# Modulation slots 8 and up moved from the token projection to the mixers' front, and the two widest masked copies made by ScalarE

## The reference, cut to what matters

```
mod = silu(c) @ w_mod + b_mod            # one row per group: shift, scale, gate (twice), 6 x 1024
h   = rmsnorm(x) * (1 + sc1) + sh1
z   = h @ w_in                            # 2352 columns: latents of the attention, q, k, v, gates of the recurrences
o   = [attention(z), hgrn2(z), gla(z)]    # the three mixers
x   = x + g1 * (o @ w_o)
h2  = rmsnorm(x) * (1 + sc2) + sh2
x   = x + g2 * ((silu(a) * u) @ w_ffn_out),   a, u = h2 @ w_ffn_in
```

## Time and profile before

| | |
|---|---|
| median of 3 runs | 3438.68 us (3432.39 to 3442.31) |
| profiled execution, its own time | 3439.55 us |
| its span, first to last instruction | 3437.7 us |
| PE busy | 3216.9 us, 94% of the span |
| mean granted TensorE clock | 0.975 of full speed |
| token projection of layer 0, of layer 1 | 140.4 to 340.1 us, 1831.4 to 2018.4 us |
| mixers' front of layer 0, of layer 1 | 340 to 444 us, 2018 to 2122 us |

### The profile page before, as it was taken

The page is one execution under the profiler, slowest core; times in us unless marked ns, Lnnn a source line. Parts: engine busy times, 40 slices in busy tenths (PEclk is TensorE's granted clock), DMA queues, the critical chain, the costliest instruction groups (busy, mean ns, idle before and its releaser), DMA issues. The chain is left out here.

```text
span 3437.7 us, 50868 instructions
## 1 busy us (share of the span) xinstructions
PE 3216.9 (94%) x19854; PEld 2901.5 (84%) x19854; DVE 1488.5 (43%) x2525; ACT 983.0 (29%) x2015; POOL 762.6 (22%) x1091
## 2 busy tenths in 40 slices
PE   6999788889999999999989987888899999999999
PEld 5988556666999999999988975666589999999998
DVE  5411446655353334433372124566555334333443
ACT  4212334444331111111152123444434121211211
POOL 4101757631210000000051155665213000000000
PEclk7999999999999999999999999999999999999999
DMA  6565111103111111111125431110221111111111
GB/s 210 183 194 172 55 45 58 39 15 105 62 38 49 37 37 49 50 48 37 37 87 172 148 89 52 46 53 21 61 93 37 37 37 61 49 37 37 37 37 52
DMA packets 191693, 237.04 MB, mean 69 GB/s; under 512 B 18058, under 2 KB 165855, under 8 KB 191551
## 3 DMA queue, kind: packets, MB, share of 16 engines
q1 hardware_dynamic: 176764, 198.29, 17.9%
q0 software_dynamic: 10560, 31.44, 2.7%
q10 hardware_dynamic: 4226, 5.40, 0.6%
HBM read 195.53 MB, written 39.56 MB: 68 GB/s over the span
## 5 line engine op out<-in xcount | busy, mean ns | idle before, releaser
L1560 PE MATMUL banks<-act_split,w_split 128*128 128x384 f32 (+1 forms) x8352 | 1403.6, 329 | 10.6 <-DVE act_split L2293 7.4
L1560 PEld LDWEIGHTS banks<-act_split,w_split 128*128 128x128 f32 x8352 | 1387.0, 189 | 23.2 <-DVE act_split L2293 12.3
L1560 PE MATMUL banks<-hidden_split,w_split 128*128 128x384 f32 (+1 forms) x3168 | 525.0, 326 | 0.0
L1560 PEld LDWEIGHTS banks<-hidden_split,w_split 128*128 128x128 f32 x3168 | 522.3, 188 | 0.0
L2330 DVE SCALAR_TENSOR_TENSOR x<-banks,mod,x 128x384 f32<-128x384 f32 (+2 forms) x768 | 353.4, 497 | 185.6 <-PE banks L1560 183.2
L2768 DVE TENSOR_TENSOR hidden_f<-banks,silu_a 128x384 f32<-128x384 f32 x132 | 70.7, 536 | 736.5 <-PE banks L1560 736.5
L1560 PE MATMUL banks<-w_split_tm,act_split 128*128 128x396 f32 (+1 forms) x1728 | 323.9, 345 | 0.0
L1560 PEld LDWEIGHTS banks<-w_split_tm,act_split 128*128 128x128 f32 (+1 forms) x1728 | 299.2, 182 | 25.6 <-issue 14.0
L1521 ACT ACTIVATE w_split<-w_raw 128x2048 fp32r<-128x2048 f32 x60 | 112.4, 1906 | 381.3 <-PE banks L1560 381.3
L1515 ACT ACTIVATE hidden_split<-hidden_f 128x384 fp32r<-128x384 f32 x132 | 67.1, 508 | 519.6 <-DVE hidden_f L2768 519.6
L621 POOL TENSOR_TENSOR norm_sum_n<-norm_sum_n,norm_sq 128x384 f32<-128x384 f32 (+1 forms) x42 | 43.9, 1048 | 771.8 <-ACT norm_sq L972 766.6
(11 more groups left out here) (233 smaller groups left out, 3424.2 us busy)
## 6 DMA issues: line engine op xcount, KB each, us to landing
w_raw<-in_w_ffn_in SPq DMA_DIRECT2D x44, 1024.0 KB, 5.1
w_mod_raw<-in_w_mod SPq DMA_DIRECT2D x41, 1024.0 KB, 5.4
w_raw<-in_w_ffn_out SPq DMA_DIRECT2D x22, 1024.0 KB, 4.9
z_token_major<-z_stage POOLq DMA_DIRECT2D x64, 198.0 KB, 2.4
r_qkg<-z_feature_major SPq DMA_DIRECT2D x16, 576.0 KB, 4.2
r_v<-z_token_major SPq DMA_DIRECT2D x16, 512.0 KB, 3.6
w_raw<-in_w_o SPq DMA_DIRECT2D x8, 1024.0 KB, 7.1
w_mod_first<-in_w_mod SPq DMA_DIRECT2D x7, 1024.0 KB, 12.4
```

The costliest lines, as they stand in the source:

```text
L1560: return T.matmul(out, lhsT, rhs, start=start, stop=stop, skip_group_check=True)
```

## The change

1. Slots 0 to 7 of layer 0 stay where they are. All others leave the token projection, on PE, DVE and SP. In the front, step i carries slot 8 + i: PE runs `mod_turns(i)` between its piece and `r_slot(i)`, or before the piece in steps 6, 7, 11, 15, 19 and 23. DVE runs the copy and the keeping at the end of its step i. PSUM banks 2 and 3 take the place of 6 and 7 there.
2. The weights of a slot come in two DMAs of 512 KB, into two buffers of their own (`w_mod_front`). Slot 8 is loaded by SP early in the token projection; all others are issued by ACT: slot 9 as the front begins, slot 10 + i at the end of ACT's step i, once PE has made the rows of slot 8 + i.
3. Levels 5 and 6 (b = 32, 64) of all 9 tiles are copied from PSUM to r_p by ACT, in two plain copies of 32 partitions x 256 elements and one of 64 x 512, in place of DVE's two masked copies of 128 x 512 (`wide_level`, in ACT's steps h = 6 and 7). PE's `outputs` and the next users of their banks wait for ACT accordingly.
4. PE waits at the end of the front for the last slot to be kept, and ACT's first softmax exponential for the last rows. SP, POOL and DVE no longer wait for the slots before the front.

```
+WIDE_LV = 5
...
+    def load_mod(eng, l, n):
+        s = 8 + n
+        src = w_mod_v[l + s // NMOD][:, :, 256 * (s % NMOD):256 * (s % NMOD) + 256]
+        for u in range(2):
+            eng.dma_start(MF[n % 2][u].rearrange("p (k c) -> p k c", k=4), src[:, 4 * u:4 * u + 4]).then_inc(mod_ld[n % 2], 16)
...
-                order = [("t", 0), ("t", 1)] + mods[:2] + [("t", 2)] + mods[2:4] + [("t", 3)] + mods[4:11]
-                order += [("w", 9), ("w", 10)] + mods[11:17] + [("w", 11)] + mods[17:]
+                order = [("t", 0), ("t", 1), ("m", 0), ("t", 2), ("t", 3), ("w", 9), ("w", 10), ("w", 11)]
...
+                def wide_level(g, lv):
+                    b = LEVELS[lv]
+                    src = ps[R_BANK[f"s{lv}"]].rearrange("p (h n c) -> p h n c", h=8, c=b)
+                    wait(act, "r_pe", l, f"s{g}_{lv}")
+                    wait(act, "r_dve", l, f"m{g}_{WIDE_LV - 1}")
+                    for n in range(64 // b):
+                        t0 = 2 * b * n
+                        ins = S.activation(rP[t0:t0 + b, :, t0 + b:t0 + 2 * b], src[t0:t0 + b, :, n], ACT.Copy)
...
                     if i:
                         r_slot(i)
+                    if i + 2 < NMOD_L[l]:
+                        act.wait_ge(mod_pe, l * NMOD + 8 + i + 1)
+                        load_mod(S, l, i + 2)
...
-                        pos = 9 * j + p
-                        if pos < 33 and pos % 4 < 3:
-                            mod_turns(pos - pos // 4)
...
                 for i in range(24):
+                    ahead = i == 6 or i % 4 == 3 and i > 3
+                    if ahead:
+                        mod_turns(i)
...
+                    if not ahead:
+                        mod_turns(i)
                     if i:
                         r_slot(i)
+                mod_turns(24)
+                pe.wait_ge(mod_dve, MOD_ALL[l])
...
-                    if g < NTILE and h:
+                    if g < NTILE and 0 < h <= WIDE_LV:
                         masked(g, h - 1)
...
                         k_sum(f"p{(i - 9) // 4}", P)
+                    mod_parts(i)
+                mod_parts(24)
```

More of the change, by code:

```diff
@@ L196, in program @@
     at = [h_at, h_end]
-    MR = place("w_mod_raw", [P, 2, 2048], F32, at)
-    MS = place("mod_rows", [P, 256], F32, at)
+    MR = place("w_mod_raw", [P, 2048], F32, at)
+    MS = place("mod_rows", [P, 256], F32, [h_at + 16384, h_end])
     CST = place("cst", [P, CST_W], F32)
@@ L262, in program @@
     rQB = place("r_qb", [P, 2, 8, 64], F32, a)
+    MSF = place("mod_rows_front", [P, 256], F32, a)
     a = [wr_at + 6144, wr_at + SLOT * 4]
@@ L285, in program @@
     PT = place("probs_t", [P, 2, 4, P], F32, a)
+    MF = [[place(f"w_mod_front{i}{u}", [P, 1024], F32, [o, o + 4096])
+           for u, o in enumerate((h_at, h_at + 4096) if i == 0 else (h_at + 8192, a_at + 43008))] for i in range(2)]
     CT = place("c_t", [P, 4, P], F32, a)
@@ L455, in _ @@
                     load_raw(l, n, wl[:, :, FM_COLS[n]:FM_COLS[n] + 256], 8)
-                mods = [("m", n) for n in range(8, 8 + NMOD_L[l])]
-                order = [("t", 0), ("t", 1)] + mods[:2] + [("t", 2)] + mods[2:4] + [("t", 3)] + mods[4:11]
-                order += [("w", 9), ("w", 10)] + mods[11:17] + [("w", 11)] + mods[17:]
+                order = [("t", 0), ("t", 1), ("m", 0), ("t", 2), ("t", 3), ("w", 9), ("w", 10), ("w", 11)]
                 for kind, n in order:
                     if kind == "m":
[L462 to L466, removed]
+                        wait(sp, "n1_dve", l, "lo27")
+                        load_mod(sp, l, n)
                     elif kind == "t":
@@ L1096, in r_slot @@
                     if g < NTILE:
+                        if h > WIDE_LV:
+                            wide_level(g, h - 1)
                         if h == 0:
@@ L1208, in probs @@
                     wait(act, "a_dve", l, f"mx{t}_{h}")
+                    if q == 0 and h == 0:
+                        act.wait_ge(mod_pe, MOD_ALL[l])
                     if h >= 2:
@@ L1283, in _ @@
                 t8, n8 = ORDER[0], DEC_SEQ
+                load_mod(S, l, 1)
                 decay(0, 0, 0)
@@ L1581, in mod_rows @@
                 def mod_rows(q):
[L1583 to L1586, removed]
-                    else:
[L1588 to L1591, removed]
+                    first = l == 0 and q < 8
+                    if first:
+                        pe.wait_ge(mod_la[q] if q < NMOD_A else mod_l7, 16)
+                        w = [(MA[:, q] if q < NMOD_A else MR)[:, 1024 * u:1024 * u + 1024] for u in range(2)]
+                        bank = ps[3 if q % 2 else 6]
+                    else:
+                        pe.wait_ge(mod_ld[q % 2], mod_ready(l, q - 8))
+                        w, bank = MF[q % 2], ps[2]
                     if q > first:
@@ L1595, in mod_rows @@
                         g = 32 * (k % 4)
-                        ins = mm(ps[3 if first and q % 2 else 6][g:g + 32, 0:256], SCV[:, k, :], w[:, k, :], k < 4, k >= 4)
+                        ins = mm(bank[g:g + 32, 0:256], SCV[:, k, :], w[k // 4].rearrange("p (k c) -> p k c", k=4)[:, k % 4],
+                                 k < 4, k >= 4)
                     ins.then_inc(mod_pe, 1)
@@ L1603, in mod_turn @@
                         pe.wait_ge(mod_dve, l * NMOD + q)
+                    first = l == 0 and q < 8
                     for ct in range(2):
-                        ins = mm(ps[7][:, 2 * ct:2 * ct + 2], MS[:, P * ct:P * ct + P], CST[:, O_SEL:O_SEL + 2],
-                                 True, True)
+                        ins = mm(ps[7 if first else 3][:, 2 * ct:2 * ct + 2], (MS if first else MSF)[:, P * ct:P * ct + P],
+                                 CST[:, O_SEL:O_SEL + 2], True, True)
                     ins.then_inc(mod_sum, 1)
@@ L1785, in outputs @@
                     b = R_BANK["o"]
-                    wait(pe, "r_dve", l, f"m{g}_{NLEV - 1}")
+                    wait(pe, "r_dve", l, f"m{g}_{WIDE_LV - 1}")
+                    wait(pe, "r_act", l, f"m{g}_{NLEV - 1}")
                     pe.wait_ge(rv_ld, (l * NTILE + g + 1) * 16)
@@ L2367, in mod_copy @@
                         dve.wait_ge(mod_sum, l * NMOD + q)
-                    V.tensor_copy(MS[:], ps[3 if l == 0 and q < 8 and q % 2 else 6][:, 0:256]).then_inc(mod_ev, 1)
+                    if l == 0 and q < 8:
+                        V.tensor_copy(MS[:], ps[3 if q % 2 else 6][:, 0:256]).then_inc(mod_ev, 1)
+                    else:
+                        V.tensor_copy(MSF[:], ps[2][:, 0:256]).then_inc(mod_ev, 1)
                 def mod_keep(q):
                     dve.wait_ge(mod_sum, l * NMOD + q + 1)
+                    src = ps[7 if l == 0 and q < 8 else 3][:, 0:4].rearrange("p (k a) -> p k a", k=2)
                     if q >= NMOD:
-                        V.tensor_copy(MODN[:, 2 * (q - NMOD):2 * (q - NMOD) + 2, :],
-                                      ps[7][:, 0:4].rearrange("p (k a) -> p k a", k=2)).then_inc(mod_dve, 1)
+                        V.tensor_copy(MODN[:, 2 * (q - NMOD):2 * (q - NMOD) + 2, :], src).then_inc(mod_dve, 1)
                         return
-                    V.tensor_tensor(MOD[:, 2 * q:2 * q + 2, :], ps[7][:, 0:4].rearrange("p (k a) -> p k a", k=2),
+                    V.tensor_tensor(MOD[:, 2 * q:2 * q + 2, :], src,
                                     PRM[:, 2 * q:2 * q + 2].unsqueeze(2).broadcast_to([P, 2, 2]), ALU.add).then_inc(mod_dve, 1)
@@ L2424, in gate, with mod_parts @@
                     s.done(V.tensor_scalar(ZT3[:, 0:n], ZT3[:, 0:n], 1.0 / TAU, None, ALU.mult), f"g{c}")
-                for p in range(25):
+                def mod_parts(p):
                     if 1 <= p <= NMOD_L[l]:
@@ L2430, in _ @@
                         mod_copy(8 + p)
[L2431 to L2434, removed]
+                split_lo(l, 5, None)
+                split_lo(l, 6, None)
+                for c in range(3):
+                    gate(c)
                 rs = st("r_dve")
                 s = st("a_dve")
-                dve.wait_ge(mod_dve, MOD_ALL[l])
                 def rstep(ins, name, now=False):
```

17 lines of the change are left out of this document (7 added, 10 removed).

## The result

| | before | changed |
|---|---|---|
| median | 3438.68 us | 3459.49 us (3456.76 to 3461.1) |
| profiled execution, its span | 3437.7 us | 3459.3 us |
| mean granted clock | 0.975 | 0.971 |

The ratio is 1.006, with a 95% interval of 1.0045 to 1.0074: the changed kernel is slower by 20.8 us. Forecast were 3436 us with a range up to 3456, so the forecast was wrong.

What follows compares the result with a forecast made beforehand. PE was taken to bound the kernel, busy 3216.9 of 3437.7 us. From 3439.55 us, 58.4 removed and 55.9 taken back by the fronts gave 3437.0, by the median 3436 us, with a range from 3410 to 3456.

Steps and rivals of the forecast that it cites:

- What is removed: Token projections: 24 slots leave layer 0 and 16 leave layer 1, 35.0 + 23.4 = 58.4 us, all on the path.
- The walk of the tile: Front, steps 8 to 15: eight slots worth 11.7 us cost 12.8 us, as a longer PE-DVE-PE loop leaves gaps unfilled.
- a slot is 1.46 us on PE: Front: each slot's turn and rows priced at a mean of 1.46 us on PE.
- The rest of step 15 runs at half clock before and warm behind shorter gaps: 1 us back: Front, end of the tile: late by 13.8 us at k_turn, 1 us won back, so step 16 starts 12.8 us late.
- rival 2: Fronts: slots shorten long waits, so up to half of 38 us at half rate is won, 9 us: 3427 us; chance 0.09.
- The sum: Whole kernel: 3439.55 - 58.4 removed + 55.9 taken back by the fronts = 3437.0, so 3436 us by the median.
- the first tile of layer 1: Front of layer 1, first tile: slots add 8 us, the figure walked for the first tile of layer 0.
- a front over 145 us: Sign of being wrong: fronts exceeding 145 us, and then, by PE's wait on w_mod_front, Rival 3 holds.
- The masked copies: Attention: 36 copies leaving DVE, partly for ACT, costed at nothing; bounds 18 us gained to 14 us lost.
- Rival 1: Fronts grow only by what exceeds the gaps, 7.6 us and nothing: 3388 us, halfway 3412; chance 0.20.
- Rival 3: `mod_rows` in the front: loads landing in 7.4 us instead of 5.4 add 20 us, 3456 us; chance 0.28.

Runs made afterwards that it cites:

- changed_again: The changed kernel itself run once more, unaltered, beside the other runs: 3456.5 us, 1.0054 times the kernel before.
- filled: The changed kernel with 2 to 7 useless matmuls of 256 columns put into PE's waits ahead of turns in the front: 3435.1 us, ratio 0.9992.
- wide_only: The kernel before with only levels 5 and 6 copied by ACT, no slots moved: 3438.9 us, ratio 0.9997.
- sooner_masked: copy_first_sooner with levels 5 and 6 back as masked copies on DVE: 3402.1 us, ratio 0.9903.
- copy_first_sooner: The changed kernel with DVE's slot copy first in its step and ACT's loads issued ahead of ACT's recurrence part: 3405.6 us, ratio 0.9905.

## Why the prediction was wrong, step by step

**What is removed** was right: 62.3 us where 58.4 were forecast, 1.54 to 1.56 us per slot in place of 1.46.

**The walk of the tile** had the right mechanism and the right waits. The level of step 9 came 3.2 us late (forecast 3.1). The turn of step 10 waited 3.46 us for a copy behind k_sum, that of step 11 waited 2.20, of step 14 1.22, of step 15 2.04, all at the places named. The step that failed is the price of what stands behind these waits: "a slot is 1.46 us on PE", a level 1.1, k_turn 0.9, all at full rate. The levels of steps 10, 11, 13 and 14 came 8.1, 12.7, 16.8 and 19.2 us late, forecast 7.0, 9.4, 12.3 and 15.0. The error arises in step 10 (1.1) and step 11 (2.2 more), where rows, levels and k_turn take 1.76 to 1.94 us each, 1.2 more come up to step 13, where the level of step 11 is still at half rate, and about 1 more in step 15. Step 16 started 18.1 us late, forecast 12.8. In the profile of changed_again the same 3.3 us arise in steps 10 and 11 and nothing is added behind them: step 16 started 15.4 us late. In filled, where the same order of work runs at a clock of 1.00, the tile takes 46.5 us: 11.8 more than before, against the 12.8 of the walk. So the loop of PE and DVE was read well to 1 us in this tile, and the clock made 6.3 us of it (3.5 in changed_again).

**"The rest of step 15 runs at half clock before and warm behind shorter gaps: 1 us back"** did not come in the first profile: the gap ahead of k_turn did shrink from 4.78 to 2.04 us, and k_turn still ran at half rate (1.94 us). In changed_again it ran at full rate (1.08 us) behind the same 2.04 us. So this term is a matter of the execution, and small. The clock was in the walk only there, where it helped. It was not asked what the new waits of 2 to 3.5 us would do, although the text on rival 2 said that the walk "puts waits of 2 to 4 us in new places".

**The sum** was short by 87.0 - 55.9 = 31.1 us in the fronts, less 3.9 from the removal and 3.1 from the rest. Against the kernel before, the two fronts grew by 87.0 us in the first profile of the changed kernel, by 78.7 in changed_again and by 61.2 in filled (139.2 and 127.3 us long). So half rate behind the waits is 26 or 18 us by the profiles and 21 by the medians. The 5.3 us between 61.2 and 55.9 are the first tile of layer 1. Growth by tile in filled is 8.5, 11.8 and 15.1 us in layer 0, forecast 8, 12.8 and 13.8; in layer 1 it is 13.1, 11.8 and 0.9, forecast 8, 12.8 and 0.5. The prediction took the first tile of layer 1 to be like that of layer 0, but before it was 34.4 us long and not 36.8, and in filled 47.6 and not 45.2. Why it took in the slots less well stays open.

The prediction's own sign of being wrong, a front over 145 us, came in layer 0, but without the wait on w_mod_front that it had tied to it: none of its three rivals was this case.

**The masked copies** at nothing: right within what can be measured, by wide_only and by sooner_masked. The 4.7 and -5.2 us in the rests of the layers are of both signs.

**Rival 1, the gaps take the slots in** (0.20), is false for the changed kernel and about half true for copy_first_sooner: there the slots lengthen the front of layer 0 from 103.8 to 117.7 us and that of layer 1 from 101.4 to 116.2, 28.6 us for the 62.3 us that the projections lost, where the rival had 7.6. For the most part the gaps were not bound to a loop as such; the place of the copy made them so.

**Rival 2, the clock comes back**, is the right quantity with the wrong sign in layer 0: 0.92 fell to 0.85 (0.88 in changed_again). In layer 1 it hardly moved, 0.90 to 0.89 (0.93 in changed_again). The Trainium skill, "TensorE: Matmul & The Clock Gate", Part 1, was drawn on for more matmuls meaning more clock. The rows say that the matmuls added did not raise it in layer 0, since the waits that they brought with them lowered it; with these waits filled it was 1.00.

**Rival 3, the loads pace the front**, was right on the side and wrong on the cause. They landed in 3.6 to 10.5 us, median 4.6, and PE never waited for them. The figure that the prediction took from the Trainium skill, "DMA: Bandwidth & Descriptors", Anatomy of one DMA, is given there for DMAs that GpSimd issues; the ones here are issued by SP and ACT, so only the rows speak for them. The loads are a true bound only behind the first one: once the copy stands first, they cost 20 us, ACT's issuing included.

## What to carry to other kernels

When work with a hand-off to another engine is moved into a loop, put the other engine's part at the head of its step, where its input is ready, and not at the end behind work that starts later; here that one line decides between 0.5% slower and 0.5% faster. When you walk a loop, price what follows a new wait both at full and at half rate: in the changed kernel's first profile the rows of a slot took 1.4 to 1.9 us behind 12 of 13 waits of 1.7 to 3.5 us, and 1.07 behind one. Check the sum of PE's busy time afterwards: here it grew by 19.6 us, and by 6.6 in the second profile, with the same count of matmuls, the sign that more of them ran at half rate. Then look for the second bound right away, since the loads that were harmless in the slower version were worth 15 to 20 us in the faster one.

## What was unexpected

- Useless matmuls in the waits made the kernel 21 us faster (3456.5 to 3435.1 us), with 129.1 us of busy time for 979 matmul records against 128.7 for 880.
- Waits as short as 1.7 to 2.2 us were followed by half rate in some places (rows of 1.93 us behind 1.73 at 449.97 in the changed kernel) and not in others (rows of 1.07 us behind 2.04 at 344.62 in the same profile). What PE had done before them differs; which of it decides was not tried.
- Two profiles of the same changed kernel differ by 4.6 us in the front of layer 0 (162.2 and 157.6 us from the last z_stage copy to the first softmax exponential), at clocks of 0.85 and 0.88.
